# A two-block kernel: products inside the first normalisation, the upper parts on ScalarE, GpSimd for the second head's normalising, shorter routing

## The reference

```python
# block 1
h = rmsnorm(x, g_mix); z = h @ w_in         # mLSTM q/k, v, o, gates; neighbourhood qkv; memory q; branch gates
h_m   = mlstm(silu(conv(qk)), v, i, f), forward and backward
h_na  = softmax(q_na @ window(k_na) + rpb) @ window(v_na)   # 8 heads x 32, window 8 rows x 16 columns of 64
h_mem = softmax(rms(q_mem) @ rms(k)) @ v    # k, v from rmsnorm(mem, g_mem) @ w_mem_kv, 256 tokens, 4 heads x 64
x = x + (gates * (h_m, h_na, h_mem projected)) @ w_out
x = x + square(relu(rmsnorm(x, g_ffn) @ w_up)) @ w_down     # 4096 wide
# block 2
x = x + concat(gated_delta_net(h), retention(h)) @ w_out_2
g = argmax(h2 @ w_router_group)             # 1 of 8 groups, then the top 2 of its 8 experts
x = x + sum over the 2 experts of weight * (silu(h2 @ w_gate[e]) * (h2 @ w_up[e])) @ w_down[e]   # 64 experts, 256 wide
out = rmsnorm(x, final_norm)
```

## Time and profile before

| | us |
|---|---|
| median of 3 runs | 3116.68 (3116.31 to 3117.28) |
| the profiled execution: its own time | 3113.51 |
| its span | 3110.6 |
| PE busy | 2816.0 (91%) |
| DVE busy | 1289.7 (41%) |
| ACT busy | 593.7 (19%) |
| POOL busy | 347.3 (11%) |

### The profile page before, as it was taken

How to read it: one execution, slowest core, us unless ns; L and a number is a source line. 1 busy time by engine, 2 the same in 40 slices (tenths; PEclk the granted TensorE clock), 3 DMA queues, 4 the chain that set the end, 5 groups by cost and what they waited for, 6 DMA issues and landing times. The chain is left out here.

```text
span 3110.6 us, 42264 instructions
## 1 busy us (share of the span) xinstructions
PE 2816.0 (91%) x17384; PEld 2201.4 (71%) x17384; DVE 1289.7 (41%) x2196; ACT 593.7 (19%) x1446; POOL 347.3 (11%) x486
## 2 busy tenths in 40 slices
PE   7987888999999999999999998889999868888882
PEld 5866755888877888888887886777888745545451
DVE  5647378233355424243345653554434431111114
ACT  3233167010002101000002322331012201111111
POOL 1013200000001000000001002441011111111112
PEclk8989999999999999999999998999999979999997
DMA  3120130111131111111114320002112189999994
GB/s 131 55 80 26 41 104 23 41 55 36 50 119 33 63 42 41 54 41 62 41 48 112 48 46 1 2 2 55 41 31 106 64 343 416 416 414 409 402 387 187
DMA packets 131743, 362.90 MB, mean 117 GB/s; under 512 B 14808, under 2 KB 61016, under 8 KB 114144
## 3 DMA queue, kind: packets, MB, share of 16 engines
q1 hardware_dynamic: 120336, 341.70, 30.5%
q0 software_dynamic: 10512, 16.80, 1.5%
q10 hardware_dynamic: 704, 1.70, 0.1%
HBM read 349.21 MB, written 31.52 MB: 122 GB/s over the span
## 5 line engine op out<-in xcount | busy, mean ns | idle before, releaser
L460 PE MATMUL banks<-hT_upper,split_weights 128*128 128x512 f32 x2304 | 717.8, 391 | 8.8 <-DVE split_weights L137 4.4
L460 PEld LDWEIGHTS banks<-hT_upper,split_weights 128*128 128x128 f32 x2304 | 434.1, 188 | 100.0 <-issue 4.9
L451 PE MATMUL banks<-split_weights,hT_upper 128*128 128x512 f32 x1536 | 483.4, 396 | 18.7 <-DVE hT_lower L137 7.9
L460 PE MATMUL banks<-hT_lower,split_weights 128*128 128x512 f32 x1152 | 449.8, 390 | 0.0
L451 PEld LDWEIGHTS banks<-split_weights,hT_upper 128*128 128x128 f32 x1536 | 291.3, 191 | 81.4 <-issue 14.3
L451 PE MATMUL banks<-split_weights,uT_upper 128*128 128x512 f32 x1024 | 315.6, 389 | 0.0
L3052 PE MATMUL banks<-expert,ex_xT 128*64 128x256 f32 (+1 forms) x1632 | 263.8, 400 | 44.3 <-DMA expert<-in_w_up 19.9
L451 PE MATMUL banks<-split_weights,hT_lower 128*128 128x512 f32 x768 | 303.5, 395 | 0.0
L460 PEld LDWEIGHTS banks<-hT_lower,split_weights 128*128 128x128 f32 x1152 | 217.0, 188 | 44.8
L3052 PEld LDWEIGHTS banks<-expert,ex_xT 128*64 128x64 f32 (+1 forms) x1632 | 171.3, 150 | 100.9 <-issue 60.8
L451 PEld LDWEIGHTS banks<-split_weights,uT_upper 128*128 128x128 f32 x1024 | 191.9, 188 | 39.6
(11 more groups left out here) (483 smaller groups left out, 3682.7 us busy)
## 6 DMA issues: line engine op xcount, KB each, us to landing
expert<-in_w_gate SPq DMA_DIRECT2D x51, 1024.0 KB, 13.0
expert<-in_w_up SPq DMA_DIRECT2D x51, 1024.0 KB, 22.5
expert<-in_w_down SPq DMA_DIRECT2D x50, 1024.0 KB, 24.7
raw_weights<-in_w_in SPq DMA_DIRECT2D x38, 1024.0 KB, 6.0
raw_weights<-in_w_up SPq DMA_DIRECT2D x16, 1024.0 KB, 5.3
raw_weights<-in_w_down SPq DMA_DIRECT2D x16, 1024.0 KB, 5.0
hT<-in_w_gate SPq DMA_DIRECT2D x13, 1024.0 KB, 11.6
hT<-in_w_up SPq DMA_DIRECT2D x13, 1024.0 KB, 22.5
```

The lines of the kernel that those rows point to most:

```text
L451: last = pe.matmul(bank, acts[x][:, r * KT // 2 + k, m * P:(m + 1) * P].bitcast(F32R), w[y][:, k, :].bitcast(F32R), start=(r == 0 and k == ...
L460: last = pe.matmul(out, w[x][:, k, c0:c0 + P].bitcast(F32R), acts[y][:, k, t0:t0 + nt].bitcast(F32R), start=(k == 0 and x == y), stop=(k = ...
```

## The change

In `first_norm` the transposes go to banks 4 to 7. DVE's split of the chunk and of the gate weights stands before tile 4. PE has a second list, `ahead()`: the 24 gate products of the first half of the tokens, then the 48 of the first two channel groups, on banks 0, 2 and 3. It takes eight of the list after each tile from 5 on, and what is left at the end. `mlstm_inputs` then has 24 gate products and six channel groups left, its groups in another order.

In `attention_inputs` the casts of hT and of the memory rows are made by ACT, and DVE waits for them. In `attention` DVE multiplies the first head of a neighbourhood unit and POOL the second; PE's turn waits for both. In `route` the eight and the 16 products of 64 columns become one on DVE and two on POOL, M comes from the sum of the two one-hots of 8 experts, the count from a sum of M over the tiles, the running sums go to POOL, and PE makes the rank products behind the order's.

```diff
+    XS, XN, NB, SOON = 3, 2, 4, 4
...
-                if i == n_split:
+                if i == SOON:
                     c.split_chunk(dve, C_QK)
                     dve.wait_ge(others_landed, 16 * len(others))
-                    split(dve, nc.vector, V, c.k["w_if"], w_if[0], w_if[1])
+                    split(dve, nc.vector, V, c.k["w_if"], w_if[0], w_if[1]).then_inc(w_if_split, 1)
...
+            def ahead():
+
+                pe.wait_ge(copied, 2 * SOON)
+                pe.wait_ge(w_if_split, 1)
+                yield from gate_products(nc.tensor, c, hT, w_if, 0)
+                c.wait_split(pe, C_QK)
+                for ch in range(2):
+                    yield from early_products(nc.tensor, c, hT, ch)
+
+            soon = ahead()
...
-                        last = nc.tensor.transpose(c.bank(b % NB)[:, k * P:(k + 1) * P],
+                        last = nc.tensor.transpose(c.bank(NB + b % NB)[:, k * P:(k + 1) * P],
...
+                if i > SOON:
+                    for _ in itertools.islice(soon, 8):
+                        pass
+            for _ in soon:
+                pass
+
+
+def gate_products(pe, c, hT, w_if, th):
+
+    for k in range(KT):
+        for x, y in PASSES:
+            yield pe.matmul(c.psum[0:WIDTH, th, :], w_if[x][:, k, :].bitcast(F32R),
+                            hT[y][:, k, th * BANK:(th + 1) * BANK].bitcast(F32R),
+                            start=(k == 0 and x == y), stop=(k == KT - 1 and x == 1))
...
+def early_products(pe, c, hT, ch):
+
+    w = c.parts(C_QK)
+    for k in range(KT):
+        for x, y in PASSES:
+            yield pe.matmul(c.bank(2 + ch), w[x][:, k, ch * P:(ch + 1) * P].bitcast(F32R), hT[y][:, k, 0:BANK].bitcast(F32R),
+                            start=(k == 0 and x == y), stop=(k == KT - 1 and x == 1))
...
+        QK = [(2 * half + a, th) for half in range(2) for th in range(2) for a in range(2)]
+        EARLY_QK = 2
...
-            for th in range(2):
-                for k in range(KT):
-                    for x, y in PASSES:
-                        last = nc.tensor.matmul(c.psum[0:WIDTH, th, :], w_if[x][:, k, :].bitcast(F32R),
-                                                hT[y][:, k, th * BANK:(th + 1) * BANK].bitcast(F32R),
-                                                start=(k == 0 and x == y), stop=(k == KT - 1 and x == 1))
-                last.then_inc(product, 1)
-            for i in range(8):
-                j = C_QK + i // 4
-                if i % 4 == 0:
+            for last in gate_products(nc.tensor, c, hT, w_if, 1):
+                pass
+            last.then_inc(product, EARLY_QK + 2)
+            for i in range(EARLY_QK, 8):
+                ch, th = QK[i]
+                j = C_QK + ch // 2
+                if i == 4:
                     c.wait_split(pe, j)
                 if i >= 6:
                     pe.wait_ge(rows_taken, i - 6 + 1)
-                split_channels(nc.tensor, c.bank((i + 2) % 8), hT, i % 2 * BANK, BANK, c.parts(j), i // 2 % 2 * P).then_inc(product, 1)
+                split_channels(nc.tensor, c.bank((i + 2) % 8), hT, th * BANK, BANK, c.parts(j), ch % 2 * P).then_inc(product, 1)
...
+            for m in range(TT):
+                cols = slice(m * P, (m + 1) * P)
+                nc.scalar.activation(hT[0][:, :, cols].bitcast(F32R), whole[:, :, cols], ACT.Copy).then_inc(h_upper, 1)
+            nc.scalar.activation(mem_parts[0].bitcast(F32R), memT, ACT.Copy).then_inc(h_upper, 1)
...
-                split(dve, nc.vector, V, whole[:, :, cols], hT[0][:, :, cols], hT[1][:, :, cols]).then_inc(h_split, 1)
+                dve.wait_ge(h_upper, m + 1)
+                take_lower(nc.vector, hT[1][:, :, cols], whole[:, :, cols], hT[0][:, :, cols]).then_inc(h_split, 1)
                 if m == 2:
                     c.split_chunk(dve, C_NAQK + 1)
-            split(dve, nc.vector, V, memT, mem_parts[0], mem_parts[1]).then_inc(mem_split, 1)
+            dve.wait_ge(h_upper, TT + 1)
+            take_lower(nc.vector, mem_parts[1], memT, mem_parts[0]).then_inc(mem_split, 1)
...
+                if units[u][0] == "na":
+                    pe.wait_ge(second_normed, na_before(u + 1))
...
-                for j in range(2):
+                for j in range(2 if units[u][0] == "mem" else 1):
                     p = sc[:, u % NS, j, 0:w]
                     ins = nc.vector.tensor_scalar(p, p, rden[:, u, j:j + 1], None, ALU.mult)
                 ins.then_inc(normed, 1)
...
+        @block.gpsimd
+        def _(pl):
+            for u in range(n):
+                if units[u][0] == "na":
+                    pl.wait_ge(rden_ready, u + 1)
+                    p = sc[:, u % NS, 1, :]
+                    nc.gpsimd.tensor_scalar(p, p, rden[:, u, 1:2], None, ALU.mult).then_inc(second_normed, 1)
...
+            nc.gpsimd.memset(earlier[:, 0, :], 0.0).then_inc(begun, 1)
             nc.gpsimd.memset(experts.xg[:, :, :], 0.0).then_inc(cleared, 1)
+            pl.wait_ge(picks_ready, 1)
+            for m in range(TT):
+                pl.wait_ge(begun, m + 1)
+                last = nc.gpsimd.tensor_tensor(earlier[:, m + 1, :], earlier[:, m, :], M[:, m, :], ALU.add)
+                last.then_inc(begun if m < TT - 1 else earlier_ready, 1)
+            for k, oh in enumerate((oh1, oh2)):
+                nc.gpsimd.tensor_tensor(groups(OH[:, k, :, :]), in_group(goh), in_all_groups(oh), ALU.mult).then_inc(OH_ready, 1)
             pl.wait_ge(cleared, 1)
...
-            pe.wait_ge(picks_ready, 1)
-            nc.tensor.matmul(c.bank(4), c.k["mask_lt"][:, :], M[:, :, :].rearrange("p t e -> p (t e)"), start=True, stop=False)
-            pe.wait_ge(earlier_ready, 1)
-            nc.tensor.matmul(c.bank(5)[:, 0:E], ones[:, :], earlier[:, TT, :], start=True, stop=True)
-            nc.tensor.matmul(c.bank(5)[0:E, E:E + 1], earlier[:, TT, :], ones[:, 0:1], start=True, stop=True).then_inc(counted, 1)
-            nc.tensor.matmul(c.bank(4), ones[:, :], earlier[:, 0:TT, :].rearrange("p t e -> p (t e)"), start=False, stop=True).then_inc(ranked, 1)
+            pe.wait_ge(sum_ready, 1)
+            nc.tensor.matmul(c.bank(5)[:, 0:E], ones[:, :], Msum[:, :], start=True, stop=True)
+            nc.tensor.matmul(c.bank(5)[0:E, E:E + 1], Msum[:, :], ones[:, 0:1], start=True, stop=True).then_inc(counted, 1)
             pe.wait_ge(perm_ready, 1)
             nc.tensor.matmul(c.bank(6)[0:1, 0:E], c.k["iota_p"][0:E, 0:1], perm[0:E, :], start=True, stop=True).then_inc(order_there, 1)
+            pe.wait_ge(earlier_ready, 1)
+            nc.tensor.matmul(c.bank(4), c.k["mask_lt"][:, :], M[:, :, :].rearrange("p t e -> p (t e)"), start=True, stop=False)
+            nc.tensor.matmul(c.bank(4), ones[:, :], earlier[:, 0:TT, :].rearrange("p t e -> p (t e)"), start=False, stop=True).then_inc(ranked, 1)
...
-            for m in range(TT):
-                V.done(v.tensor_tensor(tmp[:, m, :].rearrange("p (g e) -> p g e", g=NG),
-                                       lg[:, m, NG:GR].rearrange("p (g e) -> p g e", g=NG),
-                                       goh[:, m, :].unsqueeze(2).to_broadcast([P, NG, PG]), ALU.mult))
-            V.settle(dve)
+            do(v.tensor_tensor(groups(tmp[:, :, :]), groups(lg[:, :, NG:GR]), in_group(goh), ALU.mult))
...
-            for m in range(TT):
-                for k, oh in enumerate((oh1, oh2)):
-                    V.done(v.tensor_tensor(OH[:, k, m, :].rearrange("p (g e) -> p g e", g=NG),
-                                           goh[:, m, :].unsqueeze(2).to_broadcast([P, NG, PG]),
-                                           oh[:, m, :].unsqueeze(1).to_broadcast([P, NG, PG]), ALU.mult))
-            V.settle(dve)
-            do(v.tensor_tensor(M[:, :, :], OH[:, 0, :, :], OH[:, 1, :, :], ALU.add))
-            for m in range(TT):
-                ins = v.tensor_tensor(earlier[:, m + 1, :], earlier[:, m, :], M[:, m, :], ALU.add)
-                if m == 0:
-                    dve.sem_inc(picks_ready, 1)
-                if m < TT - 1:
-                    do(ins)
-            ins.then_inc(earlier_ready, 1)
+            do(v.tensor_tensor(both[:, :, :], oh1[:, :, :], oh2[:, :, :], ALU.add))
+            v.tensor_tensor(groups(M[:, :, :]), in_group(goh), in_all_groups(both), ALU.mult).then_inc(picks_ready, 1)
+            dve.wait_ge(picks_ready, 1)
+            v.tensor_reduce(Msum[:, :], M[:, :, :].rearrange("p t e -> p e t"), AX.X, ALU.add).then_inc(sum_ready, 1)
...
+            dve.wait_ge(OH_ready, 2)
```

More of the change, by code:

```diff
@@ L1 @@
+import itertools
 import math
@@ L218, in wait_consts, with first_norm @@
     eng.wait_ge(c.consts_landed, 16 * c.n_consts)
-def first_norm(c, name, tiles, n_split, upper, needed, others, w_if):
-    nc, n = c.nc, len(tiles)
-    XS, XN, NB = 3, 2, 4
+def first_norm(c, name, tiles, n_split, hT, needed, others, w_if):
+    nc, n, upper = c.nc, len(tiles), hT[0]
+    XS, XN, NB, SOON = 3, 2, 4, 4
     with ExitStack() as mem:
@@ L269, in uppers @@
```

(4 more changed lines are left out.)

20 lines of the change are left out of this document (16 added, 4 removed).

## The result

| | before | changed |
|---|---|---|
| median, 20 runs each | 3117.22 us (3114.86 to 3122.33) | 3121.99 us (3118.04 to 3132.57) |
| profiled execution, span | 3110.6 | 3119.9 |
| POOL busy | 347.3 | 411.6 |

The ratio is 1.0019, with an interval of 1.0013 to 1.0026: 4 to 8 us slower. 3106.8 was forecast, and the range ended at 3113. The changed kernel's times also spread more: 12 of 20 lie between 3118.0 and 3123.5, eight between 3125.4 and 3132.6.

The account below looks back on a forecast made before the run. The prediction took the expert stage as bound by its transfers and TensorE as the engine with the most work ahead of it. Its terms, -7.1 - 2.85 + 2.1 - 2.0 = -9.9, took 3116.68 to 3106.8 us, range 3102 to 3113.

Parts of the forecast that it names:

- the price of GpSimd's head: Attention: POOL's 128x512 multiplication takes 0.64 to 0.70 us; with standing behind DVE, +0.13 a pair, +2.1 for 16 pairs.
- The sum's upper one: Whole kernel: upper bound of the summed terms, -6.4 - 2.3 + 2.4 - 0.8 = -7.1, giving 3109.6 us.
- The prediction's own sign of being wrong: Prediction is wrong if the clock stays low in the interleaved stage, or POOL's rows are longer than 1 us throughout.
- The first rival: Attention: POOL's head costs like the two-input row and stands behind DVE, +8 to +11, total about 3113 to 3116; 12%.
- The lock: Attention: POOL stands until DVE's first head is through, ending 1.05 after the reciprocal, against 0.8 alone.
- First normalisation: First stage: 72 products moved among the transposes let the next stage begin 6.4 to 8.0 us earlier, taken as -7.1.
- the thin margin of PE behind DVE: First normalisation: DVE has tile 9 ready at about 35.7, PE asks for it at about 36.1 or later.
- the time at the lower level: First normalisation: 3 to 6.5 us of the interleaved stretch at PE's lower clock, adding 1.4 to 3.0 us.
- The rival in which the clock stays down: First normalisation: the interleaved stage doesn't raise the clock, +7.8 in place of -7.1, total 3121.8; 3% or so for slower.
- Splitting the rows: Before attention: casts go from DVE to ACT, so the first unit's reduction comes 2.85 us earlier (2.3 to 3.3).
- Routing: Routing stage: the count's copy comes 3.5 us earlier, of which 2.0 is taken as gain, between 0.8 and 3.5.
- The sum: Whole kernel: -7.1 - 2.85 + 2.1 - 2.0 = -9.9, 3106.8 us against the median of 3116.68.

Follow-up runs that it names:

- experiment 4: Kernel of experiment 1 plus four scratch multiplications on GpSimd at the very start, while DVE has nothing to do; 3106.44 us in its one run.
- experiment 3: Changed kernel with GpSimd's multiplication written as a product of two tensors, the reciprocal broadcast; 3115.28 us, ratio 0.999 to the kernel before.
- experiment 2: Kernel before with only GpSimd normalising the second head of the neighbourhood units; 3143.04 us, ratio 1.0081.
- experiment 6: Kernel before with the first normalisation's part of the change alone; 3108.02 us, ratio 0.9972.
- experiment 7: Kernel before with the casts of the normalised rows on ACT alone; 3116.16 us, ratio 0.9996.
- experiment 1: Changed kernel without GpSimd's head, DVE normalising both heads in the attention; 3106.32 us, ratio 0.9967 to the kernel before.

## Why the prediction was wrong

**The term that failed is the price of GpSimd's head.** "I take 0.64 to 0.70, since the operation has one large input": the three rows were an affine select, a product of two tensors and a tensor_scalar of 16 elements, and the value came from the nearest by the count of inputs. The form itself takes 1.58 (experiment 4), and 1.86 in its place. The working around it was right: the end of the second head moved from 0.92 after the reciprocal to some 2.0 (1.86, started 0.1 after it), a pair by +1.06, and 16 pairs by +16.2, where +2.1 stood. The bounds failed with it. The sum's upper one had +2.4 for this term, and 1.05, the dearest row of an operation of this size, stood only in a rival; a bound from other instructions bounds only those. The prediction's own sign of being wrong, rows of POOL longer than 1 us throughout, is what came. The first rival, "POOL's head costs like the two-input row and stands behind DVE as well: +8 to +11", was measured as experiment 3: +10.0 (137.3 against 127.3), though it is DVE that stands there. It had 12% and was still 6 short.

**The lock** was taken in the right direction for this form, and about in its size: the working let GpSimd's head end at 1.05 after the reciprocal instead of 0.8, 0.25 of standing, and 0.28 was measured. The Trainium skill (SBUF — State Buffer, "Who interferes with whom") has the port pair as an exclusive lock that blocks the other for a whole instruction. The traces agree that one of the two stands, but not always for the whole: DVE's head was held for 0.93 by GpSimd's 1.04, GpSimd's for 0.28 by DVE's 0.49. Its sentence that issue order decides who blocks does not fit experiment 3, where DVE started 0.05 ahead and was the one that was held. In the changed kernel DVE starts ahead by 0.06 as well, and there GpSimd is held; what differs between the two is GpSimd's form.

**A second loss was not in the forecast at all.** The stall of PE costs more than its length where the clock falls with it: 26 us in experiment 2 against 16 in the changed kernel, with 0.91 of granted clock in the attention. Only one profile shows it. Why the two profiles of the changed kernel are free of it, with the same stalls, is open.

**First normalisation: mechanism right, size low.** -7.1 (to -8.0) was forecast, -9.1 came. DVE's order, tile 5 at 26.5 (26.29) and the thin margin of PE behind DVE (0.4, measured 0.45, both some 2 later) were right. The upper level was there from about 28, as the first of the placed products began, and stayed while they filled the gaps; that they raised it is argued from the four profiles with the old stage, which reach it at about 40 and 46. The term that was off is the time at the lower level, 3 to 6.5 us from tile 5's start, which was 1.7 (26.29 to 28.0; up to 3.7 in experiment 6); at the next block's start PE waited 0.30 and not 1.05. The 0.71 of the first window in the earlier trace rows was read too high: the column gives 1.00 for the first 16 us, in which two tiles took 1.57 each. The rival in which the clock stays down is refuted by the products at 0.23 each from 28 on.

**Splitting the rows: right for the stage,** -2.85 forecast, -2.8 and -3.0 in the changed kernel and in experiment 7. The way there was partly luck. The first reduction came only 1.9 earlier, since the squares came 1.3 later after the stage's start and not 0.3: PE's first products there ran at the lower level for 5.4 us, against 3.2 before. PE's waits for DVE's normalised rows fell from 7.6 to 4.8 over the stage, as much as the stage gained.

**Routing: right in most steps,** the count 3.5 earlier, the running sums 3.10 for eight, the two products 2.10, the experts' first product -2.0. The first weights were taken as 3.5 earlier too and are asked for only 2.3 earlier (14.1 after the routing's start, 16.4 before). Between the count's copy and the copy of the order DVE took 3.60 instead of 2.37, with three small operations held beside GpSimd's: 0.40 for 0.25, 0.75 for 0.25, 0.72 for 0.15. The prediction had such a delay, 1 to 1.5, but only on the way to the tokens' table. How much reaches the end is open.

**The sum.** Without GpSimd's term, the forecast was 3116.68 - 7.1 - 2.85 - 2.0 = 3104.7, and 3106.3 was measured (experiment 1). With its measured +16 it would have been 3120.9, and 3121.99 came. That the three other terms fit so well is in part luck: their stages gained 13.9 and not 12.0, the medians 10.8, and that median is known to some 4 us only (6 to 14).

## What to carry to other kernels

A price for GpSimd must come from the same instruction at the same size. Its forms differ by 2.5 for one and the same number of elements (0.64, 1.04, 1.58), and not in the order of their inputs; where no row has the form, the upper bound is open, and the range has to say so. Where an engine waits for two pieces of work in a row, hand over the first when it is done before giving the second to another engine: here the one cost 16 us and the other gained 3.5 between medians, 5.7 in the stage. Products placed into a stage that waits for a chain of short steps fill its gaps; here the upper clock also came earlier with them, at 28 to 30.4 and not at 40 to 46.

## What the runs showed of the hardware

- GpSimd, 128 x 512 fp32 with DVE silent: 1.58 us for a multiplication by a scalar from SBUF, 1.50 by an immediate, 1.04 for two tensors (one a broadcast). 128 columns take 0.60.
- DVE and GpSimd multiplying at once: with GpSimd's form of one tensor, GpSimd is held (1.86 for 1.58), DVE hardly (0.49 for 0.44). With its form of two tensors, DVE is held (1.37 for 0.44) and GpSimd not at all (1.04).
- With two operations of DVE's (0.93 for both), GpSimd's 128 columns take 1.01 for 0.60.
- Beside GpSimd's sums and products of two tensors in the routing, small operations of DVE's take 0.40, 0.75 and 0.72 us where they took 0.25, 0.25 and 0.15.
- With PE idle for 1.7 us in every pair of units, the granted clock in that stage was 0.91 in one profile (experiment 2) and 1.00 in the two of the changed kernel, 8 us apart.
- The granted clock was given as 1.00 in a window where eight transposes took 1.57 us, their length where the granted clock reads 0.50; at the upper level they take 0.86.
